# A recurrence done chunk by chunk in PSUM, softplus moved ahead of the pooling, sample taps of the long convolution among the merges, key selection in PSUM

## The chip, the cores and the metric

The program runs on one NeuronCore of a Trainium2 chip. Its engines are TensorE (PE in the profile, with PEld for its weight loads), VectorE (DVE), ScalarE (ACT), GpSimd (POOL) and SyncE (SP), which issues the loads. The metric is the device time of one execution in microseconds; lower is better.

## The reference, cut to what matters

Two layers of a hybrid decoder run over 256 prompt rows and 8 x 4 sample rows, 288 columns in all. In each layer an input projection feeds four mixers, their outputs are gated and merged, and a product-key expert layer (PEER) follows.

```python
# mixer B: trailing means over 2/4/8/16 tokens, minus the token, then a linear per group
# mixer C
xconv = causal_dwconv(ext, w_conv) + b_conv                      # 4 taps, 1024 channels
r  = sigmoid(xh @ w_a + b_a);  ig = sigmoid(xh @ w_i + b_i)
log_a = -8 * r * softplus(-lam);  a = exp(log_a)
bx = sqrt(-expm1(2 * log_a)) * (ig * xconv)
h_t = a_t * h_(t-1) + bx_t                                       # the recurrence
yc = h * gelu(yg)
# mixer D: z = val * sigmoid(gate); 31-tap causal convolution; LayerNorm; silu
# PEER: s = q . keys; top 16 of each half; 16 x 16 sums; top 16 of these;
i1 = take(si[0], pos // 16); i2 = take(si[1], pos % 16); expert = 128 * i1 + i2
```

## The kernel before, in words

Activations lie with channels on the 128 partitions and the 288 columns along the free side. Weights stream from HBM as tiles of 128 output channels: SP loads a tile `raw` (512 KB) into a ring of four. For every half of a tile (4 of 8 blocks of 128x128) ACT writes a rounded high part `w_high`, POOL subtracts it to make `w_low` (line 544), and PE does 12 matmuls of 288 columns (lines 610 to 612: high x high, high x low, low x high). So one tile needs, in this order, two ACT copies, two POOL subtractions and 24 matmuls, and ACT's copy for tile n+2 waits until PE has finished the same half of tile n. ACT also takes each finished tile out of PSUM in order.

The order of all this is written out by hand, per engine, with semaphores: every engine runs its own list in order. In a layer the sections of tiles are B (4 tiles), C (16), S (20 small products with the pool and LRU weights), D (8), A (12), then XB, XC and XA (each pairs of a gate tile and a branch tile), DG, DP, OUT, WQ, U0, KEYS, the U groups and the V groups.

DVE's list in the part that is changed: the norm; wait for B; the pooling of mixer B in four channel groups (lines 1222 to 1236, then the split into `pb_high` and `pb_low`); the argument of softplus (1241, 1243); wait for eight C tiles; the four taps of conv C in PSUM, its sample columns, and the split of `xconv` in four pairs of chunks, each of which raises `c_conv` (line 1258); the softplus series, 24 instructions on 128x8 (1262 to 1283); the split of `y_b`; the products for the recurrence on all eight chunks at once (1290 to 1294); mixer D's gating and sample columns (1297 to 1194); one scan over 2304 elements (1315) and its followers (1317 to 1203); then taps of conv D, most of them between the merges (line 1337) of XB and XC.

PE starts S with waits for `pooled` and for the first `c_conv`. ACT computes the exponential of softplus after its fourth C tile, having waited for DVE's argument (line 911). During D it does Exp and Tanh of each chunk, during A one Sqrt over all chunks (962). `conv_samples` multiplies the window of each sample by the taps and sums.

`route` picks the experts for 128 rows at a time, three times a layer, while PE runs the U groups. With `eq` in SBUF it compares 128 positions with 16 numbers (1517), multiplies by the indices (1520) and sums (1523), each on 128x2048.

Of the kernel before, what the change touches and what calls it, by code (L numbers as in the profile page):

```python
# [37 lines left out]
P = 128  # L38
# [123 lines left out]
def build(nc, w_first, x_in, params_in, final_in, pool_first, ext_in, h0_in, w_in, w_pool, w_lru, w_ab, w_c, w_d, w_out,  # L162
          w_q, w_keys, w_u, w_v, x_keep, y_out, ext_out, h_out):
    with ExitStack() as ctx:
# [140 lines left out]
        lru_exp, lru_ratio, lru_root, y_ready = (sem(n) for n in ("lru_exp", "lru_ratio", "lru_root", "y_ready"))  # L305
        merges_done, chunk_summed, chunk_high = (sem(n) for n in ("merges_done", "chunk_summed", "chunk_high"))
# [149 lines left out]
        with nc.Fori(0, DEPTH) as layer:  # L456
            with nc.Block() as block:
# [146 lines left out]
                def _(pe):  # L604
# [103 lines left out]
                    pe.wait_ge(extra_out, 20)  # L708
# [158 lines left out]
                def _(act):  # L867
# [35 lines left out]
                    for s in range(RING):  # L903
                        into_ext("b", "B", 0, s, s)
                    for g in range(2):
                        for s in range(RING):
                            into_ext("c", "C", g, s, 4 * g + s)
                        if g == 0:

                            act.wait_ge(softplus_arg, 1)  # L910
                            A(lru[:, 1, :], lru[:, 0, :], ACT.Exp, scale=-1.0).then_inc(softplus_exp, 1)
# [28 lines left out]
                    def tanh_of(c0):  # L940
                        for c in (c0, c0 + 1):

                            act.wait_ge(lru_a, c + 1)
                            last = A(rg[:, c, :], rg[:, c, :], ACT.Tanh, scale=lru[:, 7, c:c + 1])
                        return last

                    for s in range(RING):
# [3 lines left out]
                        if s > 0:  # L951
                            last = tanh_of(2 * s - 2)
                    last = tanh_of(CC - 2)
                    last.then_inc(lru_exp, 1)
# [191 lines left out]
                def _(dve):  # L1146
# [22 lines left out]
                    def conv_samples(m, out, bias, scratch, spot):  # L1169
# [3 lines left out]
                        col = PCOL["conv_" + m]  # L1173
                        w, b = spot[:, 0:taps * n], spot[:, taps * n:taps * n + n]
                        did(V.tensor_copy(w, par[:, col:col + taps * n]))
                        if bias:
                            did(V.tensor_copy(b, pcol(bias, 0, n)))
# [3 lines left out]
                        sets = max(1, min(TS, 1152 // size))  # L1181
                        product = [scratch[:, i * size:(i + 1) * size].rearrange("p (c b j) -> p c b j", c=n, b=NB)
                                   for i in range(sets)]
                        s_out = by_seq_all(out)
                        for t0 in range(0, TS, sets):
                            for t in range(t0, t0 + sets):
                                did(V.tensor_tensor(product[t - t0], e[:, :, :, t:t + taps], w, ALU.mult))
                            settle()
                            for t in range(t0, t0 + sets):
                                did(V.tensor_reduce(s_out[:, :, :, t], product[t - t0], AX.X, ALU.add))  # L1190
                            settle()
                        if bias:
                            for t in range(TS):
# [18 lines left out]
                    norm_scale(dve, 0, par[:, PCOL["norm1"]:PCOL["norm1"] + KC])  # L1212
                    dve.wait_ge(padded, 1)
# [27 lines left out]
                    did(V.tensor_scalar(lru[:, 0, :], pcol("lam", 0, CC), -1.0, None, ALU.mult))  # L1241
                    settle()
                    V.tensor_tensor(lru[:, 0, :], lru[:, 0, :], pcol("lam", 0, CC), ALU.max).then_inc(softplus_arg, 1)

# [6 lines left out]
                    conv_samples("c", xconv, "conv_c_b", yb_flat, bank[4])  # L1251
# [9 lines left out]
                    dve.wait_ge(softplus_exp, 1)  # L1261
                    did(V.tensor_scalar(lru[:, 2, :], lru[:, 1, :], 2.0, None, ALU.add))
                    settle()
                    did(V.reciprocal(lru[:, 2, :], lru[:, 2, :]))
                    settle()
                    did(V.tensor_tensor(lru[:, 3, :], lru[:, 1, :], lru[:, 2, :], ALU.mult))
                    settle()
                    did(V.tensor_tensor(lru[:, 4, :], lru[:, 3, :], lru[:, 3, :], ALU.mult))
                    settle()
                    did(V.tensor_scalar(lru[:, 5, :], lru[:, 4, :], 2.0 / 17, 2.0 / 15, ALU.mult, ALU.add))  # L1270
                    for k in (13, 11, 9, 7, 5, 3, 1):
                        settle()
                        did(V.tensor_tensor(lru[:, 5, :], lru[:, 5, :], lru[:, 4, :], ALU.mult))
                        settle()
# [481 lines left out]
```

## Time and profile before

| | us |
|---|---|
| median of 3 runs (lowest, highest) | 2899.95 (2898.25, 2900.65) |
| the profiled execution | 2899.97 |
| its span in the trace | 2898.1 |
| PE, PEld busy | 2670.1, 2621.1 |
| POOL, DVE, ACT busy | 2233.1, 1637.9, 1384.3 |

Times in the rows are counted from the span's start. "Idle before" is how long the engine sat idle ahead of an instruction, with what ended that. PE's matmuls overlap: one lasts 0.30 us and the next starts 0.13 us after it at the full clock, so an idle time read from the profile is 0.17 us shorter than the time that the stall costs.

### The profile page before, as it was taken

Reading aid. Unit: us, or ns where it says so; the run is one execution under the profiler, and the core shown is the slowest. Engines: PE = TensorE matmul, PEld = TensorE weight load, DVE = VectorE, ACT = ScalarE, POOL = GpSimd, SP = SyncE. Lnnn points to the kernel's source line nnn. Section 1 sums busy time; section 2 is a strip of 40 time slices with the busy share of each in tenths; the row PEclk is TensorE's granted clock in tenths of the full one; section 3 lists DMA queues with packets and bytes.
Section 4 is the critical chain, followed back from the end, with each engine's and each line's share of the span. In section 5 each row is a group of like instructions: output and inputs, shape, how many; then the busy total and the mean of one; then the engine's idle time right before and its main releaser. Section 6 shows DMA issues by size and latency. Waiting matters only on the chain. (4 is left out here: it accounts for less than half of the span.)

```text
span 2898.1 us, 58908 instructions
## 1 busy us (share of the span) xinstructions
PE 2670.1 (92%) x19546; PEld 2621.1 (90%) x19546; DVE 1637.9 (57%) x3379; ACT 1384.3 (48%) x2689; POOL 2233.1 (77%) x1819
## 2 busy tenths in 40 slices
PE   7889999999778999999978898999997799999997
PEld 6889889999668999999878898999996699999997
DVE  4686234993885344333656852259928843443336
ACT  4654544445223455554646545444442244554555
POOL 5888667998767878888757876679986678788886
PEclk8999999999999999999989999999999999999999
DMA  4445554454113555555444456545551135555553
GB/s 157 137 137 162 150 167 144 151 160 154 52 38 104 164 154 166 182 166 164 143 137 141 135 156 162 160 139 159 152 152 37 45 123 161 158 161 183 166 166 128
DMA packets 126244, 411.09 MB, mean 142 GB/s; under 512 B 20016, under 2 KB 24496, under 8 KB 125360
## 3 DMA queue, kind: packets, MB, share of 16 engines
q1 hardware_dynamic: 120160, 403.38, 45.3%
q10 hardware_dynamic: 5968, 6.22, 0.9%
q8 instruction: 66, 1.08, 0.2%
q14 instruction: 50, 0.41, 0.0%
HBM read 403.32 MB, written 6.22 MB: 141 GB/s over the span
## 5 line engine op out<-in xcount | busy, mean ns | idle before, releaser
L544 POOL TENSOR_TENSOR w_low<-raw,w_high 128x512 fp32r<-128x512 f32 x1450 | 1987.1, 1379 | 520.3 <-ACT w_high L875 446.4
L875 ACT ACTIVATE w_high<-raw 128x512 fp32r<-128x512 f32 x1266 | 797.0, 633 | 1044.7 <-PE bank L612 1030.0
L610 PE MATMUL bank<-xn_high,w_high 128*128 128x288 f32 x3456 | 1046.6, 303 | 92.8 <-POOL w_low L544 61.7
L611 PE MATMUL bank<-xn_low,w_high 128*128 128x288 f32 x3456 | 1032.4, 299 | 0.0
L612 PE MATMUL bank<-xn_high,w_low 128*128 128x288 f32 x3456 | 1028.2, 298 | 0.0
L610 PEld LDWEIGHTS bank<-xn_high,w_high 128*128 128x128 f32 x3456 | 660.6, 191 | 106.3 <-POOL w_low L544 70.8
L612 PEld LDWEIGHTS bank<-xn_high,w_low 128*128 128x128 f32 x3456 | 662.0, 192 | 0.0
L611 PEld LDWEIGHTS bank<-xn_low,w_high 128*128 128x128 f32 x3456 | 661.2, 191 | 0.2
L1595 DVE TENSOR_TENSOR c_lo<-acts,c_hi 128x288 fp32r<-128x288 f32 x352 | 381.1, 1096 | 446.5 <-ACT c_hi L1089 446.5
L610 PE MATMUL bank<-c_hi,w_high 128*128 128x288 f32 x2048 | 609.1, 297 | 10.0 <-DVE c_lo L1595 9.9
L612 PE MATMUL bank<-c_hi,w_low 128*128 128x288 f32 x2048 | 605.8, 296 | 0.0
L611 PE MATMUL bank<-c_lo,w_high 128*128 128x288 f32 x2048 | 605.2, 296 | 0.0
L610 PEld LDWEIGHTS bank<-c_hi,w_high 128*128 128x128 f32 x2048 | 386.0, 188 | 17.6 <-DVE c_lo L1595 9.8
L611 PEld LDWEIGHTS bank<-c_lo,w_high 128*128 128x128 f32 x2048 | 386.0, 188 | 0.1
L612 PEld LDWEIGHTS bank<-c_hi,w_low 128*128 128x128 f32 x2048 | 385.8, 188 | 0.0
L791 PE MATMUL bank<-one,one 128*128 128x128 f32 x1152 | 167.5, 292 | 91.6 <-issue 50.7
L791 PEld LDWEIGHTS bank<-one,one 128*128 128x128 f32 x1152 | 147.6, 200 | 107.8 <-issue 57.5
L578 POOL TENSOR_SCALAR one<-iota,selT 128x128 f32<-128x128 f32 x288 | 168.0, 601 | 41.7 <-PE bank L791 39.0
L1561 DVE TENSOR_SCALAR one<-bank,selT 128x128 f32<-128x128 f32 x576 | 195.4, 401 | 0.0
L1589 DVE TENSOR_TENSOR acts<-acts,ungated 128x288 f32 x80 | 97.9, 1224 | 153.9 <-ACT ungated L889 153.8
L1098 ACT ACTIVATE w_high<-raw 128x512 fp32r<-128x512 f32 x184 | 115.7, 629 | 112.6 <-PE bank L612 112.6
L1089 ACT ACTIVATE c_hi<-acts 128x288 fp32r (+1 forms) x352 | 146.6, 430 | 22.2 <-PE bank L612 22.2
(237 smaller groups left out, 2431.8 us busy)
## 6 DMA issues: line engine op xcount, KB each, us to landing
raw<-w_u SPq DMA_DIRECT2D x256, 512.0 KB, 3.5
raw<-w_v SPq DMA_DIRECT2D x256, 512.0 KB, 3.5
raw<-w_in_t SPq DMA_DIRECT2D x136, 512.0 KB, 3.5
raw<-w_q SPq DMA_DIRECT2D x32, 512.0 KB, 3.5
raw<-w_ab SPq DMA_DIRECT2D x32, 256.0 KB, 3.1
raw<-w_c SPq DMA_DIRECT2D x16, 512.0 KB, 3.5
raw<-w_out_t SPq DMA_DIRECT2D x16, 512.0 KB, 3.8
raw<-w_first SPq DMA_DIRECT2D x12, 512.0 KB, 3.8
```

The costliest lines, as they stand in the source:

```text
L544: nc.gpsimd.tensor_tensor(w_low[slot][:, :, :], raw[s][:, 4 * half:4 * half + 4, :], w_high[slot][:, :, :].bitcast(F32), ALU.subtract)\
L578: last = nc.gpsimd.tensor_scalar(one1[1][:, t, :], iota[:, :], selT[:, 0, 4 * k + t:4 * k + t + 1], None, ALU.is_equal)
L610: nc.tensor.matmul(out, high, m_high, start=start, stop=False)
L611: nc.tensor.matmul(out, high, m_low, start=False, stop=False)
L612: return nc.tensor.matmul(out, low, m_high, start=False, stop=stop)
L791: last = nc.tensor.matmul(bank[4 + b][:, t * P:(t + 1) * P], one1[b][:, t, :], one2[b][:, t, :], start=True, stop=True)
L875: A(w_high[2 * (s % 2) + half][:, :, :], raw[s][:, 4 * half:4 * half + 4, :], ACT.Copy)\
L1089: A(c_high[:, slot, :], acts[:, i, :], ACT.Copy).then_inc(c_high_out, 1)
L1098: A(w_high[2 * (s % 2) + half][:, :, :], raw[s2][:, 4 * half:4 * half + 4, :], ACT.Copy)\
L1561: last = V.tensor_scalar(one2[b][:, t, :], hot_tiles, selT[:, 1, c:c + 1], selT[:, 2, c:c + 1], ALU.is_equal, ALU.mult)
L1589: V.tensor_tensor(acts[:, 4 * g + s, :], acts[:, 4 * g + s, :], ungated[s], ALU.mult)\
L1595: V.tensor_tensor(c_low[:, slot, :], acts[:, i, :], c_high[:, slot, :].bitcast(F32), ALU.subtract)\
```

## The change

1. The softplus argument and its whole series now stand ahead of the pooling on DVE. ACT computes the exponential right after its first B tile.
2. `ig`: ACT's sigmoid stays in PSUM, and DVE multiplies it by `xconv` from there, chunk by chunk, and only then frees the bank for PE (`extra_out`). The split of `y_b` comes after these eight products.
3. ACT computes `aa` squared into PSUM (banks 5 and 7 in turn) ahead of each Tanh; DVE forms the ratio from there chunk by chunk. Sqrt is done in eight pieces, one after each of the first eight A tiles, from `rg` into PSUM; from the third on it waits until DVE has finished the chunk two before.
4. The recurrence is done per chunk of 288 columns in PSUM: product, first sample states, scan, two copies, product with `yg`, split. It now stands ahead of mixer D's gating. PE waits for its end (`y_ready` of 2) ahead of XB.
5. Conv D: the sample columns move from the D columns to four of the XC merges; XB takes two more taps, and the loop ahead of the merges two fewer. XC's merges are written out instead of looped.
6. `route`: the comparisons, products and sums run on 128x512 pieces in banks 4 and 5, with the 16 numbers in bank 7.

```diff
@@ tensor
-                    pe.wait_ge(extra_out, 20)
+                    pe.wait_ge(y_ready, 2)
                     branch("XB", "b")
@@ scalar
                     for s in range(RING):
                         into_ext("b", "B", 0, s, s)
-                    for g in range(2):
-                        for s in range(RING):
-                            into_ext("c", "C", g, s, 4 * g + s)
-                        if g == 0:
+                        if s == 0:
 
                             act.wait_ge(softplus_arg, 1)
                             A(lru[:, 1, :], lru[:, 0, :], ACT.Exp, scale=-1.0).then_inc(softplus_exp, 1)
...
-                                    ins = A(ig[:, c, :], src, ACT.Sigmoid, bias=pcol("bi", c))
-                                ins.then_inc(extra_out, 1)
+                                    ins = A(src, src, ACT.Sigmoid, bias=pcol("bi", c))
+                                ins.then_inc(extra_out if s < 2 else ig_ready, 1)
...
                             act.wait_ge(lru_a, c + 1)
-                            last = A(rg[:, c, :], rg[:, c, :], ACT.Tanh, scale=lru[:, 7, c:c + 1])
+                            if c > 1:
+                                act.wait_ge(lru_ratio, c - 1)
+                            A(bank[5 + c % 2 * 2][:, 0:T], aa[:, c, :], ACT.Square)
+                            A(rg[:, c, :], rg[:, c, :], ACT.Tanh, scale=lru[:, 7, c:c + 1]).then_inc(lru_exp, 1)
...
-                            if (g, s) == (0, 3):
-                                act.wait_ge(lru_ratio, 1)
-                                A(rg, rg, ACT.Sqrt).then_inc(lru_root, 1)
+                            c = 4 * g + s
+                            if c < CC:
+                                act.wait_ge(lru_ratio, CC)
+                                if c > 1:
+                                    act.wait_ge(scanned, c - 1)
+                                A(bank[5 + c % 2 * 2][:, 0:T], rg[:, c, :], ACT.Sqrt).then_inc(lru_root, 1)
@@ vector
                     norm_scale(dve, 0, par[:, PCOL["norm1"]:PCOL["norm1"] + KC])
+                    did(V.tensor_scalar(lru[:, 0, :], pcol("lam", 0, CC), -1.0, None, ALU.mult))
+                    settle()
+                    V.tensor_tensor(lru[:, 0, :], lru[:, 0, :], pcol("lam", 0, CC), ALU.max).then_inc(softplus_arg, 1)
+
+                    dve.wait_ge(softplus_exp, 1)
+                    did(V.tensor_scalar(lru[:, 2, :], lru[:, 1, :], 2.0, None, ALU.add))
...
+                    V.tensor_scalar(lru[:, 7, :], lru[:, 5, :], LRU_C, None, ALU.mult).then_inc(softplus_done, 1)
...
-                    dve.wait_ge(lru_exp, 1)
-                    did(V.tensor_tensor(ig, ig, xconv, ALU.mult))
-                    settle()
-                    did(V.tensor_tensor(xconv, aa, aa, ALU.mult))
-                    settle()
-                    V.scalar_tensor_tensor(rg, xconv, 1.0, rg, ALU.add, ALU.mult).then_inc(lru_ratio, 1)
+                    for c in range(CC):
+                        dve.wait_ge(ig_ready, c + 1)
+                        V.tensor_tensor(ig[:, c, :], bank[4 + c % 4][:, 0:T], xconv[:, c, :], ALU.mult).then_inc(extra_out, 1)
+                    split(y_b, "b", y_ready)
...
+                    for c in range(CC):
+                        state = lru_bank(c)
+                        by_seq_state = by_seq(state)
+                        dve.wait_ge(lru_root, c + 1)
+                        did(V.tensor_tensor(state, state, ig[:, c, :], ALU.mult))
...
+                        did(V.tensor_tensor_scan(state, aa[:, c, :], state, 0.0, ALU.mult, ALU.add))
...
+                        did(V.tensor_tensor(state, state, yg[:, c, :], ALU.mult))
...
+                        did(V.tensor_copy(yc_high[:, c, :], state))
...
+                    V.sem_inc(y_ready, 1)
...
-                    early = CONV["d"] - 1 - 3 * KC
+                    early = CONV["d"] - 1 - 3 * KC - 2
...
+                    for c in range(KC):
+                        merge("XC", c // 2, 2 * (c % 2) + 1, [next_tap, next_tap + 1])
+                        next_tap += 2
+                        if c == 2:
+                            sample_weights("d", "conv_d_b", spot)
+                        if 2 < c < 3 + TS:
+                            conv_samples("d", cd, "conv_d_b", prod_flat, spot, c - 3, c - 2)
@@ route
-                        for c in range(2):
-                            did_r(V.tensor_tensor(e3, posf[:, c, :].unsqueeze(2).to_broadcast([P, HK, TOPK]),
-                                                iota16[:, :].unsqueeze(1).to_broadcast([P, HK, TOPK]), ALU.is_equal))
...
+                                e3 = bank[4 + q % 2][:, :].rearrange("p (s j) -> p s j", j=TOPK)
+                                did_r(V.tensor_tensor(e3, posf[:, c, h * TOPK:(h + 2) * TOPK].unsqueeze(2)
+                                                      .to_broadcast([P, 2 * TOPK, TOPK]),
+                                                      iota16_here.unsqueeze(1).to_broadcast([P, 2 * TOPK, TOPK]), ALU.is_equal))
```

On DVE, at the seam between the layer's norm and the pooling (`xn_low` is the last of the norm, `win` the window sums of the pooling), before:

```order
L371 TENSOR_TENSOR xn_low<-xnf,xn_high 128x288 x2
L1222 TENSOR_TENSOR win_99<-ext_b 128x422
L1230 SCALAR_TENSOR_TENSOR p_b<-win_99,ext_b 128x240
L1232 SCALAR_TENSOR_TENSOR p_b<-win_99,ext_b 128x32
L1234 TENSOR_TENSOR p_b<-win_99,first_cnt 128x16
```

The same place now, with the middle of the series left out:

```order
L372 TENSOR_TENSOR xn_low<-xnf,xn_high 128x288 x2
L1220 TENSOR_SCALAR lru<-par 128x8
L1222 TENSOR_TENSOR lru<-lru,par 128x8
L1225 TENSOR_SCALAR lru<-lru 128x8
L1227 RECIPROCAL lru<-lru 128x8
...
L1243 TENSOR_TENSOR lru<-lru 128x8
L1245 TENSOR_SCALAR lru<-lru 128x8
L1246 TENSOR_SCALAR lru<-lru 128x8
L1257 TENSOR_TENSOR win_99<-ext_b 128x422
L1265 SCALAR_TENSOR_TENSOR p_b<-win_99,ext_b 128x240
```

26 small instructions stand now where the pooling began at once.

On DVE, between conv C's split and mixer D's gating (`yb` is mixer B's output, `h0a` the incoming sample states), before:

```order
L1201 CAST yb_high<-y_b 128x1152
L1203 TENSOR_TENSOR yb_low<-y_b,yb_high 128x1152
L1290 TENSOR_TENSOR ig<-ig,xconv 128x2304
L1292 TENSOR_TENSOR xconv<-aa 128x2304
L1294 SCALAR_TENSOR_TENSOR rg<-xconv,rg 128x2304
L1297 TENSOR_TENSOR ext_d<-d_val,d_gate 128x4x256
L1298 TENSOR_TENSOR ext_d<-d_val,d_gate 128x4x8x4
...
L1162 TENSOR_SCALAR bank<-ext_d,par 128x256 x4
L1306 TENSOR_TENSOR ig<-ig,rg 128x2304
```

Now, to the end of the first of eight chunks:

```order
L1295 TENSOR_TENSOR ig<-bank,xconv 128x288 x8
L1208 CAST yb_high<-y_b 128x1152
L1210 TENSOR_TENSOR yb_low<-y_b,yb_high 128x1152
L1303 SCALAR_TENSOR_TENSOR rg<-bank,rg 128x288 x8
...
L1316 TENSOR_TENSOR bank<-bank,ig 128x288
L1318 TENSOR_TENSOR bank<-bank,h0a 128x8
L1320 SCALAR_TENSOR_TENSOR bank<-aa,bank 128x288
L1322 COPY h_last<-bank 128x1
L1323 COPY h_last<-bank 128x8
L1325 TENSOR_TENSOR bank<-bank,yg 128x288
L1327 CAST yc_high<-bank 128x288
L1329 TENSOR_TENSOR yc_low<-bank,yc_high 128x288
```

The instructions on 128x2304 are gone, eight groups of eight on one chunk stand in their place, and mixer D's gating comes behind all of them.

On ACT, the second tile of D, with Exp of chunks 2 and 3 and Tanh of chunks 0 and 1 (`aa` is a, `rg` is r), before:

```order
L875 ACTIVATE w_high_57<-raw_54 128x512
L875 ACTIVATE w_high_58<-raw_54 128x512
L889 ACTIVATE d_val<-bank 128x288
L950 ACTIVATE aa<-rg,lru 128x288 x2
L944 ACTIVATE rg<-rg,lru 128x288 x2
```

In the same tile now:

```order
L876 ACTIVATE w_high_57<-raw_54 128x512
L876 ACTIVATE w_high_58<-raw_54 128x512
L890 ACTIVATE d_val<-bank 128x288
L953 ACTIVATE aa<-rg,lru 128x288 x2
L947 ACTIVATE bank<-aa 128x288
L948 ACTIVATE rg<-rg,lru 128x288
L947 ACTIVATE bank<-aa 128x288
L948 ACTIVATE rg<-rg,lru 128x288
```

Two Squares into PSUM are added in each such tile.

## Rows read from the trace of the kernel before

**Rows 1.** The page's busy times, whole span

```profile
PE 2670.1 (92%) x19546; PEld 2621.1 (90%) x19546; DVE 1637.9 (57%) x3379; ACT 1384.3 (48%) x2689; POOL 2233.1 (77%) x1819
```

**Rows 2.** PE's waits in 60:70, 97:110, 125:141, 158:190 and 500:720

```profile
PE bank L610 <- POOL w_low L544: 5.1, 1, 5.1
...
PE bank L610 <- POOL w_low L544: 2.0, 2, 1.5
PE bank L610 <- ACT rg L930: 1.7, 1, 1.7
...
PE bank L610 <- POOL w_low L544: 4.4, 3, 1.7
...
PE bank L610 <- POOL w_low L544: 7.3, 4, 3.3
...
PE bank L610 <- POOL w_low L544: 8.8, 9, 1.4
```

**Rows 3.** Windows by engine: busy time, PE's granted clock, DMA

```profile
60.00:67.00 7.00, 5.14 (x21) 5.14 (x22) 0.00 (x0) 3.38 (x9) 6.05 (x5) 0.52 0.32 81
158.00:172.00 14.00, 8.92 (x56) 8.44 (x56) 13.88 (x9) 3.90 (x8) 14.00 (x6) 0.91 0.22 73
```

**Rows 4.** POOL's line 544: ns minimum/median/maximum of all its instructions

```profile
L544 POOL TENSOR_TENSOR w_low<-raw,w_high x1450: 1260/1293/5908, 28.9 to 2875.8; 128x512 fp32r<-128x512 f32 x182
```

**Rows 5.** Timeline of DVE, 125:180: start, duration, idle before

```profile
125.44 2.56 DVE L1290 TENSOR_TENSOR ig<-ig,xconv 128x2304 f32<-128x2304 f32 x1 [17.91 <-ACT rg L944]
...
162.18 5.77 DVE L1315 TENSOR_TENSOR_SCAN xconv<-aa,ig 128x2304 f32<-128x2304 f32 x1
```

**Rows 6.** Routing on DVE, 480:680, groups by form: count, busy, mean ns

```profile
L1517 DVE TENSOR_TENSOR eq<-posf,iota 128x2048 f32<-128x2048 f32 x6 | 19.8, 3298 | 0.2
```

**Rows 7.** Timeline of POOL and DVE, 47.5:49.5

```profile
47.90 1.32 POOL L544 TENSOR_TENSOR w_low<-raw,w_high 128x512 fp32r<-128x512 f32 x1 [0.21 <-ACT w_high L875]
...
47.98 1.27 DVE L1234 TENSOR_TENSOR p_b<-win,first_cnt 128x16 f32<-128x16 f32 x1
49.29 0.17 DVE L1236 TENSOR_TENSOR p_b<-p_b,ext_b 128x16 f32<-128x16 f32 x1
49.38 0.59 DVE L1222 TENSOR_TENSOR win<-ext_b 128x422 f32<-128x422 f32 x1
```

**Rows 8.** Timeline of DVE from the first pooling instruction, 38:54

```profile
38.72 1.67 DVE L1222 TENSOR_TENSOR win<-ext_b 128x422 f32<-128x422 f32 x1 [10.86 <-ACT ext_b L901]
...
50.01 3.17 DVE L1222 TENSOR_TENSOR win<-win 128x420 f32<-128x420 f32 x2
```

**Rows 9.** Timeline of DVE, conv C, its split, and softplus, 71:105

```profile
71.90 3.68 DVE L1162 TENSOR_SCALAR bank<-ext_c,par 128x256 f32<-128x256 f32 x8 [12.19 <-ACT ext_c L901]
...
91.14 1.85 DVE L1258 TENSOR_TENSOR xc_low<-xconv,xc_high 128x576 fp32r<-128x576 f32 x1
...
97.85 1.25 DVE L1262 TENSOR_SCALAR lru<-lru 128x8 f32<-128x8 f32 x1
...
104.36 0.17 DVE L1283 TENSOR_SCALAR lru<-lru 128x8 f32<-128x8 f32 x1
```

**Rows 10.** Timeline of ACT: first B tile, softplus's exponential, last C tile, D

```profile
31.23 0.19 ACT L901 ACTIVATE ext_b<-bank 128x32 f32<-128x32 f32 x1
...
59.74 0.21 ACT L911 ACTIVATE lru<-lru 128x8 f32<-128x8 f32 x1 [7.07 <-DVE lru L1243]
...
97.01 0.39 ACT L889 ACTIVATE yg<-bank 128x288 f32<-128x288 f32 x1
...
115.33 1.14 ACT L875 ACTIVATE w_high<-raw 128x512 fp32r<-128x512 f32 x2
...
117.52 0.95 ACT L944 ACTIVATE rg<-rg,lru 128x288 f32<-128x288 f32 x2
```

**Rows 11.** DVE's line 1337, one chunk with one operand in PSUM

```profile
L1337 DVE TENSOR_TENSOR bank<-bank,gates x32: 466/467/467, 233.5 to 1757.3; 128x288 f32<-128x288 f32 x32
```

**Rows 12.** DVE's waits in 500:720

```profile
DVE denom L1536 <- ACT routed L1050: 42.1, 1, 42.1
```

More of the change, by code:

```diff
@@ L904, in _ @@
                         into_ext("b", "B", 0, s, s)
+                        if s == 0:
+                            act.wait_ge(softplus_arg, 1)
+                            A(lru[:, 1, :], lru[:, 0, :], ACT.Exp, scale=-1.0).then_inc(softplus_exp, 1)
                     for g in range(2):
@@ L951, in _ @@
                         if s > 0:
-                            last = tanh_of(2 * s - 2)
-                    last = tanh_of(CC - 2)
-                    last.then_inc(lru_exp, 1)
+                            tanh_of(2 * s - 2)
+                    tanh_of(CC - 2)
                     for s in range(RING):
@@ L1167, in conv_tap, with sample_weights @@
                         return tap
-                    def conv_samples(m, out, bias, scratch, spot):
+                    def sample_weights(m, bias, spot):
+                        n, taps = CHUNKS[m], CONV[m]
+                        col = PCOL["conv_" + m]
+                        did(V.tensor_copy(spot[:, 0:taps * n], par[:, col:col + taps * n]))
+                        if bias:
+                            did(V.tensor_copy(spot[:, taps * n:taps * n + n], pcol(bias, 0, n)))
+                        settle()
@@ L1178, in conv_samples @@
-                        settle()
                         w = w.rearrange("p (j c) -> p c j", c=n).unsqueeze(2).to_broadcast([P, n, NB, taps])
                         size = n * NB * taps
-                        sets = max(1, min(TS, 1152 // size))
-                        product = [scratch[:, i * size:(i + 1) * size].rearrange("p (c b j) -> p c b j", c=n, b=NB)
-                                   for i in range(sets)]
+                        product = {t: scratch[:, (t - t0) * size:(t - t0 + 1) * size]
+                                   .rearrange("p (c b j) -> p c b j", c=n, b=NB) for t in range(t0, t1)}
@@ L1184, in conv_samples @@
                         s_out = by_seq_all(out)
-                        for t0 in range(0, TS, sets):
-                            for t in range(t0, t0 + sets):
-                                did(V.tensor_tensor(product[t - t0], e[:, :, :, t:t + taps], w, ALU.mult))
-                            settle()
-                            for t in range(t0, t0 + sets):
-                                did(V.tensor_reduce(s_out[:, :, :, t], product[t - t0], AX.X, ALU.add))
-                            settle()
+                        for t in range(t0, t1):
+                            did(V.tensor_tensor(product[t], e[:, :, :, t:t + taps], w, ALU.mult))
@@ L1192, in conv_samples @@
+                        settle()
+                        for t in range(t0, t1):
+                            did(V.tensor_reduce(s_out[:, :, :, t], product[t], AX.X, ALU.add))
+                        settle()
                         if bias:
-                            for t in range(TS):
+                            for t in range(t0, t1):
                                 did(V.tensor_tensor(s_out[:, :, :, t], s_out[:, :, :, t],
@@ L1272, in _ @@
+                    settle()
+                    did(V.memset(by_seq_all(aa)[:, :, :, 0], 0.0))
+                    did(V.memset(aa[:, :, 0:1], 0.0))
+                    yc_high, yc_low = pair["c"]
+                    for c in range(CC):
+                        state = lru_bank(c)
+                        by_seq_state = by_seq(state)
+                        dve.wait_ge(lru_root, c + 1)
+                        did(V.tensor_tensor(state, state, ig[:, c, :], ALU.mult))
                         settle()
-                        did(V.tensor_tensor(lru[:, 5, :], lru[:, 5, :], lru[:, 4, :], ALU.mult))
+                        did(V.tensor_tensor(by_seq_state[:, :, 0], by_seq_state[:, :, 0], h0a[:, c, :], ALU.add))
```

129 lines of the change are left out of this document (63 added, 66 removed).

## The prediction, made before the changed kernel ran

> **What bounds the kernel now.** The page comes first: PE is busy for 92% of the span, POOL for 77%, DVE for 57% and ACT for 48% [rows 1]. PE is the bound wherever it doesn't wait, so the question is where it waits. PE's waits, taken stretch by stretch, name POOL's `w_low` nearly everywhere: 5.1 us ahead of the seventh C tile, 2.0 in S, 4.4 in D, 7.3 in A, and 8.8 in nine pieces during routing; one more in S, 1.7, is ACT's [rows 2]. The same stretches of the second layer show the same numbers. Each piece costs 0.17 us more than it shows: 5.3, 2.3, 4.9, 8.0 and 10.3 us.
>
> POOL itself is not slow. Its median is 1.29 us, so two halves take 2.6 of the 3.2 us that a tile takes on PE; the longest is 5.9 us [rows 4]. That one starts when DVE's scan of 5.77 us runs [rows 5]. So the next view is POOL beside DVE. Where DVE works from SBUF to SBUF with two inputs, the two take turns: a DVE instruction of 16 columns started 0.08 us into a POOL one took 1.27 us and ended 0.03 us after it, while the like one behind it, with POOL idle, took 0.17 [rows 7]. Products of 2048 columns in routing take 3.3 us for the same reason, and hold POOL in turn [rows 6]. DVE's taps and merges with one operand in PSUM show no such lengthening: 466 to 467 ns, smallest to largest, though POOL works beside them [rows 11].
>
> The wait ahead of the seventh C tile is another thing: ACT stood 7.07 us in its list for the softplus argument [rows 10], which DVE makes only after its pooling. No weights were split meanwhile.
>
> After long waits PE runs at half clock for a while: granted 0.52 in 60:67, and 0.91 in 158:172 [rows 3]. Half clock spaces matmuls by 0.24 instead of 0.13 us; the 21 of 60:67 lose 2.3 us, and 0.09 x 2 x 14 = 2.5 us at half clock in A lose 1.3 us.
>
> **Routing.** The four products of 2048 columns in each third of the routing become sixteen of 512 with one operand in PSUM. They no longer take turns with POOL, and the nine waits go: 10.3 us per layer. The new time on DVE is hidden: it waits 42.1 us for ACT after its last selection [rows 12], so three times the pieces at a fixed cost of 0.1 to 0.2 us each (18 more instructions, under 4 us) are covered. If that cover were gone, nothing would change until 42 us were used.
>
> **Recurrence and A.** The scan and its five companions on 2304 columns hold POOL through A. In chunks, all but two 64-column instructions have at most one SBUF tensor, so the 8.0 us and the 1.3 us of slow clock go: 9.3 us. What comes instead is pace. ACT's Sqrt for chunk c waits for chunk c-2. A chunk takes the 0.47 us of a chunk product [rows 11] five times (two products, cast and subtraction, and the scan at 0.8, by 5.77 less a turn of about 1 us over eight), 0.2 for the sample states, 0.3 for two copies: some 3.4 us, against 3.2 per tile. The eight chunks start at tile 0 and need be kept two apart, which allows 3.2 x 7/6 = 3.7 us. So ACT never waits. PE's wait ahead of XB: the eighth chunk ends some 30 us into A, and A lasts 38.4 us. Mixer D's gating and five taps (20 instructions of about 0.45 us and 3 us of gating: 12 us) then end just as XB's first merge is due, 43 us into it. The sample columns add a product and a sum of 992 columns to each of four XC merges, some 2.5 us by the columns of [rows 11]; PE lets merges lag by two, 12.8 us, which covers all four. Nothing for these; without that cover they would cost 10 us. Bounds of this term: 6 to 10 us.
>
> **D.** The three products that held POOL there (the first is in [rows 5]) become chunk products from PSUM. The 4.9 us go. But ACT gets eight Squares in D's first four tiles. A tile there took ACT 3.04 us (from 115.33 to 118.37) with Exp and Tanh at 0.43 us each [rows 10]; two Squares at 0.35 to 0.43 make it 3.8, over PE's 3.2. ACT falls 3 us further behind, and its lead of about 1 us over the point at which POOL's second half comes late turns into one stall of 2 us. The split of `y_b` now falls beside the first D tiles and takes two turns from POOL: 0.6 us. Gain 2.3 us, bounds 0 to 4.5.
>
> **B, C and S, the part that decides.** PE no longer stands ahead of the seventh C tile: 5.3 + 2.3 = 7.6 us. DVE's wait of 10.86 us ahead of the pooling [rows 8] looks like room for the softplus series. ACT can load the table and compute Exp from 31.4 on, after the first B tile [rows 10], so the 24 small instructions start near 33. Before, they took from 97.85 to 104.5 [rows 9], 6.7 us, with POOL mostly idle. Now POOL is catching up on B and C. While it runs back to back, one small instruction fits behind each POOL one (1.25 us); by about 43.5 eleven are through. Then POOL pauses 0.2 to 0.3 us in each 1.6, and two or three fit: thirteen more take 6.5 us. The series ends near 50.
>
> The pooling follows. Of its 28 instructions, 14 ran beside POOL from 38.72 to 53.18 [rows 8], 1.03 us each; the other 14 ran in 6.5 us until 59.7 (71.90 less 12.19 [rows 9]), since POOL had nothing to do while ACT stood. That cover is gone: POOL now works throughout, so all 28 go at about 1 us. Pooling ends near 78, against 59.7. Its slack was up to the eighth C tile, which is now at 64.
>
> Conv C is then late. From its first tap to the first `c_conv` it took 71.90 to 92.99, 21.1 us [rows 9], less 2 us of turns now that POOL will run dry: `c_conv` at 97.1. PE finishes C 7.6 us sooner than before, or 7.0 with 0.6 lost at the third B tile, where the table load delays a split: at 89.9 instead of 96.9 (ACT took the last C tile at 97.01 [rows 10]). So it waits 7.2 us and starts S when it started before. The wait costs half clock again, 2.1 us, part of which S's own waits absorb; S's waits shrink by 0.5 us, as the split of `y_b` no longer meets POOL there. Net: -1.6 us per layer. Bounds: +8 (series and pooling fit) to -8 (each ten us later).
>
> **A rule weighed.** The Trainium skill, page SBUF — State Buffer, section Who interferes with whom, says that a DVE instruction with two SBUF inputs and a GpSimd one that reads SBUF exclude each other for the whole instruction, and that one with a single SBUF input outside the two-port modes doesn't contend. The trace agrees on both [rows 7, 11]. Its exclusive hold, taken to the letter with no overlap at a change of hands, is rival 2.
>
> **The sum.** Per layer 10.3 + 9.3 + 2.3 - 1.6 = 20.3; two layers 40.6. The profiled execution took 2899.97 (span 2898.1 and 1.9 around it), which is the median of the three runs within 0.02. Forecast: 2859.4 us.
>
> **Rivals.**
> 1. The series and the pooling fit into DVE's idle time. For it: 10.9 + 12.2 us of idle time stand there [rows 8, 9]. Against: the 14 instructions at 1.03 us. PE then neither waits nor slows at S: 7.2 + 2.1 + 0.6 = 9.9 per layer more: 2839.6. Chance 0.13.
> 2. No overlap at a change of hands. With POOL back to back a turn then costs 0.1 to 0.2 us more twice over, POOL's lag never drains, and one DVE instruction per POOL one is all: 21 x 1.4 = 29 us for the series, 32 for the pooling, 94 instead of 78. 16 us per layer less: 2891. Against it: 1.27 us of duration that ends 0.03 us behind POOL's with 0.17 of its own [rows 7]. By the page's letter this is the case. Chance 0.06.
> 3. The chunks set A's pace. Over 3.7 us each, PE loses seven times the excess; at 5 us 9 per layer: 2878. Chance 0.05.
> 4. Slower than before: each of the 52 instructions waits out a whole half tile, 1.6 us, as no pause is ever free. 33 + 83 = 116 for the pooling, S at 135, 38 us per layer later: 2935. It decides from 20 us per layer beyond my 78, that is a pooling that ends past 98. Against it: two instructions in one pause [rows 7]. Chance 0.05.
> 5. PSUM operands don't free POOL: DVE and POOL take turns as before: about 2899. [rows 11] speak against it. Chance 0.02.
>
> **How the numbers follow.** The forecast case has 0.69, its own range 2848 to 2871 from the bounds of its terms. The range given, 2840 to 2878, takes rival 1 at its lower end and rival 3 at its upper; outside are rivals 2, 4, 5 and edges, below 0.2. Under 0.2% (6 us) a measurement of this kernel can't tell from no change. Faster 0.92 (forecast, 1 to 3 without the tail), same 0.03, slower 0.05.
>
> **What would show it.** The wait for `c_conv` (PE idle ahead of S for 5 to 10 us, DVE as releaser) and the pooling's end near 78; no wait ahead of the seventh C tile; no PE wait on `w_low` in routing; one of some 2 us in D; none in A; POOL's maximum at 3 us or below in A. An S that starts at once, or one later than 105, makes the forecast wrong.

## The result, and the profile after

The changed kernel took 2852.85 us (median of 4 runs, 2851.45 to 2860.18), the one before 2899.1 in the same comparison (2897.24 to 2900.65). The ratio is 0.9845, interval 0.9830 to 0.9859. The forecast was 2859.4, with a range of 2840 to 2878. The profiled execution took 2853.29 us, its span 2851.4: 46.7 us off the span, where the sum had 40.6.

PE now works 93% of a shorter span, and POOL is busy for 78 us less [rows 1 for before]:

```profile
PE 2658.5 (93%) x19546; PEld 2616.8 (92%) x19546; DVE 1645.4 (58%) x3627; ACT 1392.9 (49%) x2719; POOL 2154.7 (76%) x1819
```

PE's waits answer to [rows 2]. The windows are 90:100, 100:115 and 125:141, in this order; 26:40 has 0.5 and 115:125 has 0.4 us on `w_low` besides:

```profile
PE bank L611 <- issue: 9.7, 1, 9.7
...
PE bank L611 <- POOL w_low L545: 1.5, 1, 1.5
PE bank L611 <- ACT rg L931: 0.4, 1, 0.4
...
PE bank L611 <- POOL w_low L545: 1.4, 1, 1.4
```

60:90, 141:192 and 440:705 show no wait of PE at all. The waits ahead of the seventh C tile, in A and in routing are gone, and one of 9.7 us stands ahead of S. The profile calls its releaser "issue", because the semaphore from DVE doesn't show. DVE's timeline names it: the first pair of the conv's result is split at 98.23 + 0.75 = 98.98, and PE starts S at 99.08. Timeline of DVE in the kernel after, from the softplus argument's answer to the i gate's products:

```profile
32.83 0.17 DVE L1225 TENSOR_SCALAR lru<-lru 128x8 f32<-128x8 f32 x1 [4.79 <-ACT lru L909]
...
33.47 1.23 DVE L1231 TENSOR_TENSOR lru<-lru 128x8 f32<-128x8 f32 x1
34.73 1.22 DVE L1233 TENSOR_SCALAR lru<-lru 128x8 f32<-128x8 f32 x1
...
49.97 0.16 DVE L1246 TENSOR_SCALAR lru<-lru 128x8 f32<-128x8 f32 x1
50.04 0.59 DVE L1257 TENSOR_TENSOR win<-ext_b 128x422 f32<-128x422 f32 x1
...
80.00 3.67 DVE L1167 TENSOR_SCALAR bank<-ext_c,par 128x256 f32<-128x256 f32 x8
...
98.23 0.75 DVE L1290 TENSOR_TENSOR xc_low<-xconv,xc_high 128x576 fp32r<-128x576 f32 x1
...
108.83 1.63 DVE L1295 TENSOR_TENSOR ig<-bank,xconv 128x288 f32<-128x288 f32 x4 [7.11 <-ACT bank L933]
```

An instruction on 8 columns from SBUF to SBUF takes 0.17 us alone and 1.2 where it waits for POOL. The series runs from 32.83 to 50.13, the pooling from 50.04 to 80.00. Behind the wait PE runs at half clock for a while: the window 99:107 of the kernel after shows a granted clock of 0.66. The window 158:172, in A, shows 1.00, where it was 0.91 in [rows 3]:

```profile
99.00:107.00 8.00, 7.48 (x36) 7.31 (x37) 2.73 (x5) 6.13 (x13) 1.28 (x1) 0.66 0.11 22
158.00:172.00 14.00, 14.00 (x107) 14.00 (x106) 12.98 (x35) 7.57 (x16) 11.16 (x10) 1.00 0.48 134
```

One chunk of the recurrence, and POOL's instructions from 142 to 180 (least, median, longest in ns), against the scan in [rows 5] and the 5908 ns in [rows 4]:

```profile
161.65 0.45 DVE L1316 TENSOR_TENSOR bank<-bank,ig 128x288 f32<-128x288 f32 x1
...
162.34 0.76 DVE L1320 TENSOR_TENSOR_SCAN bank<-aa,bank 128x288 f32<-128x288 f32 x1
...
164.40 0.46 DVE L1329 TENSOR_TENSOR yc_low<-bank,yc_high 128x288 fp32r<-128x288 f32 x1
164.78 0.45 DVE L1316 TENSOR_TENSOR bank<-bank,ig 128x288 f32<-128x288 f32 x1
...
L545 POOL TENSOR_TENSOR w_low<-raw,w_high x24: 1279/1292/2373, 141.1 to 177.8; 128x512 fp32r<-128x512 f32 x24
```

A chunk takes 164.78 - 161.65 = 3.13 us. In routing, the key selection's comparisons in DVE's groups of 480:700, and DVE's wait behind its last selection (window 500:720), answer to [rows 6, 12]:

```profile
L1542 DVE TENSOR_TENSOR bank<-posf,bank 128x512 f32<-128x512 f32 x24 | 15.5, 692 | 0.4
...
DVE denom L1570 <- ACT routed L1055: 40.7, 1, 40.7
```

**Where the time went.** Both traces have 19546 matmuls, so each has its partner. The table gives the start of the same matmul in both:

```
matmul, layer 1                  before   after    lead   gained since
first of D                       108.72  111.95   -3.2   -3.2  (B, C, S)
one tile behind D's last wait    137.95  138.31   -0.4   +2.9  (D)
one tile behind A's last wait    181.50  171.91   +9.6   +9.9  (A)
first of the delta gate          329.89  318.57  +11.3   +1.7
behind the last routing wait     679.65  655.27  +24.4  +13.1  (11.1 of it in the three thirds)
```

Layer 2 gives -3.3, +2.9, +10.0, +1.9 and +10.4 by the same matmuls; its three thirds of routing give 11.1 too. The slow clock behind the gate's wait is counted in the last row; with it the gate's own gain is 3.3 us in layer 1 and 1.7 in layer 2.

### The profile page after: what moved, and what is told of

The parts are those of the page before. It is cut to its first block and busy times, and to the rows that moved or that the text cites. A ratio compares the mean times of both kernels' runs of the same rounds, so it can differ in the third digit from the quotient of the medians.

```text
span 2851.4 us, 59032 instructions
## 1 busy us (share of the span) xinstructions
PE 2658.5 (93%) x19546; PEld 2616.8 (92%) x19546; DVE 1645.4 (58%) x3627; ACT 1392.9 (49%) x2719; POOL 2154.7 (76%) x1819
## 5 line engine op out<-in xcount | busy, mean ns | idle before, releaser
L545 POOL TENSOR_TENSOR w_low<-raw,w_high 128x512 fp32r<-128x512 f32 x1450 | 1908.6, 1323 | 551.9 <-ACT w_high L876 477.3
L611 PEld LDWEIGHTS bank<-c_hi,w_high 128*128 128x128 f32 x2048 | 385.5, 188 | 17.5 <-DVE c_lo L1629 10.0
```

Of the source, the lines that this page charges most:

```text
L545: nc.gpsimd.tensor_tensor(w_low[slot][:, :, :], raw[s][:, 4 * half:4 * half + 4, :], w_high[slot][:, :, :].bitcast(F32), ALU.subtract)\
L611: nc.tensor.matmul(out, high, m_high, start=start, stop=False)
```

## The experiments

Each ratio is against the kernel before on the same chip; the kernel after has 0.9845. The kernel before took 2897.47 us beside experiments 1 to 4, 2898.49 beside 5 to 8 and 2900.45 beside 9 to 11, so times of different experiments can be compared only to some 3 us. Matmul starts come from one execution of each kernel. Edits are to the kernel after where nothing else is said.

**1. The series with its scratch in a PSUM bank.** Is the series long because of POOL?

```diff
-did(V.tensor_scalar(lru[:, 5, :], lru[:, 5, :], 2.0 / k, None, ALU.add))
+did(V.tensor_scalar(ser[:, 5, :], ser[:, 5, :], 2.0 / k, None, ALU.add))   # ser is in bank 7
```

> The kernel after, with the scratch rows of the softplus series in a PSUM bank: of its 24 small instructions only one still has two SBUF inputs, the others have one operand or the result in PSUM. Theory (turns with POOL): the series took 17.2 us because POOL holds the way to SBUF; it now takes about 6 us (24 at 0.2 us, one turn), the pooling ends near 69 instead of 80.0, the first c_conv comes near 88, before PE has done with C (89.1), so PE neither waits nor slows ahead of S: 10 to 12 us per layer, 2830 us, 2826 to 2838. Rival (the series is long by its own chain of dependent instructions or by its place in the list, not by POOL): nothing changes, 2853. Half of the 24 still slow would mean that an instruction with one SBUF input and its result in PSUM takes turns too: pooling near 74, some 2843.

Measured: 2835.94 us, 0.9793 (0.9776 to 0.9809). Timeline of DVE in this kernel, and of PE's waits in 85:110 the one ahead of S:

```profile
32.83 0.17 DVE L1226 TENSOR_SCALAR bank<-lru 128x8 f32<-128x8 f32 x1 [5.84 <-ACT lru L909]
...
33.48 1.22 DVE L1232 TENSOR_TENSOR lru<-lru 128x8 f32<-128x8 f32 x1
34.73 0.17 DVE L1234 TENSOR_SCALAR bank<-lru 128x8 f32<-128x8 f32 x1
...
38.41 0.15 DVE L1247 TENSOR_SCALAR lru<-bank 128x8 f32<-128x8 f32 x1
...
88.64 1.85 DVE L1291 TENSOR_TENSOR xc_low<-xconv,xc_high 128x576 fp32r<-128x576 f32 x1
...
PE bank L611 <- issue: 1.2, 1, 1.2
```

The one instruction that keeps two SBUF inputs (L1232) is the one that still takes 1.2 us; an SBUF input with a PSUM result (L1234) takes 0.17. The series ends at 38.56 in place of 50.13, and PE starts S at 90.59 in place of 99.08. That is 8.5 us per layer, and 9.9 at the first matmul of D, where the slow clock that no longer follows is counted in. It is just under my 10 to 12: the split's first piece met POOL (1.85 us for 0.75), and 1.2 us of wait stayed. The rival falls. The medians give 16.9 us for both layers.

**2. The series back in its old place, argument and Exp early.** The block from L1224 to L1246 moves behind the conv's split.

> The kernel after, with the argument and the Exp early as now, but the series of 22 small instructions back in its old place behind the split of the conv's result. Theory: the pooling starts near 33 instead of 50 and ends near 63, c_conv is ready before PE has done with C, and PE doesn't wait ahead of S (10 to 12 us per layer). The series then runs beside POOL at about 1.2 us an instruction from 87 or so to about 105, with the i gate's products and the split of y_b behind it; D's first Exp needs it near 107. If it is in time: 2832 us; if ACT has to wait for it in D, up to 2 us per layer of that come back: 2836. Rival (the series costs its 10 us wherever it stands, once it runs beside POOL): 2853.

Measured: 2843.53 us, 0.9821 (0.9799 to 0.9843). PE starts S at 90.60, as in 1, but DVE's timeline and the longest of PE's waits in 90:112 show what follows:

```profile
94.25 1.23 DVE L1270 TENSOR_SCALAR lru<-lru 128x8 f32<-128x8 f32 x1
...
95.74 0.17 DVE L1274 TENSOR_TENSOR lru<-lru 128x8 f32<-128x8 f32 x1
...
101.92 1.54 DVE L1295 TENSOR_TENSOR ig<-bank,xconv 128x288 f32<-128x288 f32 x4
...
PE bank L611 <- DVE ig L1295: 3.6, 1, 3.6
```

POOL had caught up there, so the series took 8 us and not 18. The time is above my 2832 to 2836 all the same, because PE, in S, waits 3.6 us for the banks of the i gate, since the products that free them stand behind the series. I had looked at ACT in D as the one who waits; it was PE in S.

**3. Only the key selection changed, in the kernel before.**

> The kernel before with nothing but the key selection changed (sixteen products of 512 columns with an operand in PSUM in place of four of 2048). Theory: the nine waits of routing go, 10.3 us per layer: 2878.5 us, within 3; the waits in C, S, D, A and ahead of the first tile of the delta gate (3.8 us) stay. Rival (that stretch is helped by what the other edits do to POOL earlier): the waits stay, 2899.

Measured: 2879.06 us, 0.9931 (0.9910 to 0.9951). PE shows no wait from 500 to 710, and the first tile of the delta gate is still waited for (3.4 us between two starts). By matmul starts the three thirds gain 11.1 us in each layer, exactly as in the kernel after, so this gain is the selection's own. The medians give 18.4 us for both layers.

**4. Only recurrence, i gate's products and sample columns changed.** Softplus and key selection stand as before.

> The kernel after with softplus and key selection as in the kernel before, so that the recurrence by chunks, the i gate's products and the moved sample columns are alone. Theory: 9.3 us in A and 2.3 in D per layer, 23 in all: 2876 us. If the 1.8 us per layer by which PE waits less ahead of the delta gate's first tile, which was not forecast, belong to this part, 2872; if they belong to another part, 2876 with a wait of 3.8 us there. Rival (the gain in A comes from the time that PE lost earlier, not from the chunks): A's waits of 8 us are back, 2890 or more.

Measured: 2875.71 us, 0.9922 (0.9905 to 0.9940). PE's waits in 60:70, 125:190 and 480:700:

```profile
PE bank L611 <- POOL w_low L545: 5.1, 1, 5.1
...
PE bank L611 <- POOL w_low L545: 1.4, 1, 1.4
...
PE bank L611 <- POOL w_low L545: 8.8, 9, 1.4
```

A is free of waits and D keeps one of 1.4 us; the waits in C and in routing stay as they were in [rows 2]. By matmul starts, 1.1 us come in S, 2.9 in D and 9.9 in A: 13.9 per layer for my 11.6. The rival falls.

**5. Only argument and Exp early, in the kernel before.**

> The kernel before with only the softplus argument ahead of the pooling and its Exp behind the first B tile; series, recurrence and key selection as before. Theory: PE's wait ahead of the seventh C tile and the slow clock behind it go (7.6 us per layer), but the pooling now runs beside POOL all the way and the conv's result comes at about 90.5, so 1.5 us of wait and 1 us of slow clock come at S. The shorter wait ahead of the delta gate's first tile, seen in every kernel with the early argument (2.0 for 3.8 us), comes with it: 6.9 us per layer, 2885 us. Without that part 2889. Rival: the conv's result comes no later than before, 9.4 us per layer: 2880.

Measured: 2891.41 us, 0.9975 (0.9965 to 0.9984). The wait ahead of the seventh C tile is gone, and by matmul starts the lead over the kernel before is 6.75 us behind it and the slow clock that followed it, 5.4 at S, where 1.2 us of wait have come, and 5.5 at D's end; D shows 4.3 us of waits, as before. In layer 1 the delta gate's first tile is waited for nearly as long as before (3.64 us between two starts for 3.81), but in layer 2 it is 2.46 for 4.24. My 2885 fell, the 2889 without the shorter wait is near; whether the early argument shortens it is not settled by this run.

**6. The Squares behind D's tiles 4 to 7.**

```diff
 step("D", 1, s, d_gate[:, s, :], ACT.Sigmoid)
+for c in (2 * s, 2 * s + 1):
+    if c > 1: act.wait_ge(lru_ratio, c - 1)
+    A(bank[5 + c % 2 * 2][:, 0:T], aa[:, c, :], ACT.Square).then_inc(lru_exp, 1)
```

> The kernel after, with the eight Squares moved on ACT from D's first four tiles to behind its tiles 4 to 7, where ACT stands 0.7 to 0.9 us per tile. Theory (ACT's eight Squares of 0.40 us make the wait of 1.69 us in D): the wait goes, the one of 0.65 ahead of the first D tile stays, 1.8 us per layer: 2849 us. The last ratio comes some 2 us into A, where the first Sqrt waits for it behind the second A tile at the earliest; should ACT fall behind there, a wait of 1 to 2 us in A takes its place: 2853. Rival (the wait in D is POOL's turns with the split of y_b): it stays, 2853.

Measured: 2853.08 us, 0.9837 (0.9820 to 0.9853). PE's waits in 115:190 and in 310:320:

```profile
PE bank L611 <- POOL w_low L545: 0.4, 1, 0.4
...
PE bank L611 <- POOL w_low L545: 3.0, 1, 3.0
```

The wait of 1.4 us in D is gone, so it was the Squares', and none came in A. Nothing of it reaches the end in layer 1: ahead of the delta gate PE waits 3.0 us in place of 1.7, and that matmul starts at 318.60, with the kernel after at 318.57. In layer 2 the same wait is short, 1.84 us between two starts.

**7. The recurrence's scratch in SBUF, chunks as they are.**

```diff
-    return bank[5 + c % 2 * 2][:, 0:T]
+    return xconv[:, c, :]     # and the same in ACT's Square and Sqrt
```

> The kernel after, with the scratch of the recurrence (square, root and state of a chunk) in SBUF, in the place that the conv's result no longer needs, in place of two PSUM banks; chunks and order as in the kernel after. Theory (an operand in PSUM is what frees POOL): each of the ten instructions of a chunk then waits out a POOL one, about 1.25 us each, and holds POOL in turn; a chunk takes 10 to 13 us in place of 3.1, the loop 80 to 105 us in place of 25, and DVE is 50 to 70 us late for XB's first merge: 2950 to 2990 us. If only half of them take turns: near 2880. Rival (the gain is that the pieces are short): the chunks fit between POOL's halves, 2853 to 2857.

Measured: 2886.20 us, 0.9954 (0.9938 to 0.9971), 33 us slower than the kernel after, and far from my 2950. Timeline of DVE, of POOL and of ACT in one chunk, and PE's waits in 155:192:

```profile
158.20 0.76 DVE L1320 TENSOR_TENSOR_SCAN xconv<-aa,xconv 128x288 f32<-128x288 f32 x1
...
159.07 0.98 DVE L1323 COPY h_last<-xconv 128x8 f32<-128x8 f32 x1
160.08 1.50 DVE L1325 TENSOR_TENSOR xconv<-xconv,yg 128x288 f32<-128x288 f32 x1
...
158.73 2.53 POOL L545 TENSOR_TENSOR w_low<-raw,w_high 128x512 fp32r<-128x512 f32 x2 [2.29 <-ACT w_high L876]
...
157.69 0.44 ACT L967 ACTIVATE xconv<-rg 128x288 f32<-128x288 f32 x1 [3.07 <-DVE yc_low L1329]
...
PE bank L611 <- POOL w_low L545: 6.5, 5, 1.4
PE bank L611 <- DVEq L1332: 4.1, 1, 4.1
```

A chunk takes 4.83 us (L1325 starts at 155.26, 160.08 and 164.91). It meets two POOL instructions, not ten: ACT stands 3.07 us for the chunk two before, its splits come late, and POOL is idle for 2.29 us of each round, in which DVE's instructions with two SBUF inputs run at their own length. This is the prediction's rival 3, made real: once chunks are slower than tiles, chunk, root and weight split go round in one ring, and PE loses about 1.5 us a tile. Rival 3's own rule, seven times the excess over 3.7 us, gives 7.9 us; A's gain fell from 9.9 to 2.2, by 7.7. The 4.1 us on L1332 are PE's wait for the end of the chunks, ahead of XB. So the operand in PSUM is needed in A. My estimate failed because it let POOL run on.

**8. The key selection's pieces of 512 in SBUF.**

```diff
-e3 = bank[4 + q % 2][:, :].rearrange("p (s j) -> p s j", j=TOPK)
+e3 = eq[:, q % 2 * 512:q % 2 * 512 + 512].rearrange("p (s j) -> p s j", j=TOPK)
```

> The kernel after, with the key selection's sixteen products of 512 columns per third on SBUF tiles in place of PSUM banks. Theory: each takes a turn with POOL and holds it for 0.6 us; sixteen hold it 9 us in some 8 tiles, where it has 0.6 us to spare per tile and a buffer ahead: PE loses 2 to 3 us per third, 6 to 9 per layer: 2865 to 2872 us. Rival (short pieces are enough): no wait in routing, 2853.

Measured: 2870.82 us, 0.9895 (0.9879 to 0.9912). The size was as expected, the place was not. DVE's groups in 480:700, ACT's exponential behind the selection, PE's waits in 440:720, and DVE's wait behind its last selection:

```profile
L1542 DVE TENSOR_TENSOR eq<-posf,iota 128x512 f32<-128x512 f32 x24 | 37.1, 1585 | 0.4
...
701.44 0.52 ACT L1055 ACTIVATE routed<-routed 128x384 f32<-128x384 f32 x1 [6.88 <-DVE routed L1558]
...
PE bank L611 <- POOL w_low L545: 5.2, 1, 5.2
...
DVE denom L1568 <- ACT routed L1055: 0.6, 1, 0.6
```

The nine waits don't come back, and the three thirds gain the same 11.1 us as in the kernel after: short pieces alone let POOL keep its lead. But each of the 48 comparisons and products takes 0.9 us more (1585 for 692 ns), 44 us in all, and this uses up the 40.7 us for which DVE stood behind its last selection. ACT, which stands 6.88 us for the last selection, splits no weights meanwhile, and PE waits once, 5.2 us and its slow clock. So it was the length of a piece that freed POOL here, and the operand in PSUM that kept DVE in time.

**9. Series and last window sum in PSUM, Squares late.** The last window sum of each pooled chunk goes to `bank[5 + c % 2]`.

> The kernel with the series in PSUM (2836), and besides: the last window sum of each pooled chunk goes to a PSUM bank, so that the twelve instructions that read it have one SBUF input; and the Squares behind D's tiles 4 to 7. Theory: the pooling took 27 us from 39.36 beside POOL; its twelve readers take no turn any more, some 8 to 10 us less, so the conv's result comes near 82, 7 us before PE has done with C, and its split is over before S's turns matter. PE's wait of 1.49 us ahead of S and the slow clock in S go, 2 to 3.5 us per layer, and the wait of 1.7 in D goes, while the wait ahead of the delta gate's first tile may be 3.3 us in place of 2.2, as with the Squares alone. 2829 us, 2824 to 2834. Rival (what PE waits for at S is no longer the conv's result): 2836.

Measured: 2835.01 us, 0.9770 (0.9750 to 0.9789); not told apart from experiment 1. The stretches did what was said, if less: the conv's first piece is split at 86.2 (I had 82; the sums keep two SBUF inputs and 1.57 us each), S starts as PE ends C, 1.1 us sooner than in 1, and with D's wait gone the lead over 1 is 2.4 us behind D and 2.9 at the end of routing. Between the matmuls that start at 754 and 854 it falls to -0.2. There PE runs at half clock now and then, in other places from kernel to kernel (754:780 has a granted clock of 0.92 here and 1.00 in experiment 1); why is open. From the end of layer 1's routing to the start of layer 2, matmuls that start 0.18 to 0.30 us after the one before, for 0.13 at the full clock, lose 18.9 us here and 16.2 in experiment 1. Behind the routing of layer 2 they lose 17.5 and 14.2, and the lead is lost again. So a gain of some 3 us found early in a layer can't be seen in the time of the whole.

**10. Three of ACT's five stores early.** What does PE wait for ahead of the delta gate? Timeline of ACT's queue, kernel before and, below the dots, after:

```profile
322.75 2.73 ACTq L993 DMA_DIRECT2D ext_out_a<-ext_a  x1
325.64 2.10 ACTq L994 DMA_DIRECT2D h_out<-h_last  x1
327.87 1.15 ACT L875 ACTIVATE w_high<-raw 128x512 fp32r<-128x512 f32 x2 [6.64 <-issue]
...
313.29 1.51 ACTq L998 DMA_DIRECT2D ext_out_a<-ext_a  x1
314.97 1.44 ACTq L999 DMA_DIRECT2D h_out<-h_last  x1
316.54 1.15 ACT L876 ACTIVATE w_high<-raw 128x512 fp32r<-128x512 f32 x2 [4.79 <-issue]
```

> The kernel after, with three of ACT's five DMAs of the layer's states taken out of the place ahead of the delta gate: the ones of mixers B and C are issued beside A's tiles 9 and 10, the one of the last states behind XB. The first theory, that the shorter wait there comes with the early argument, has fallen: one kernel with it waited 3.64 us, and the kernel with the late Squares 3.33. Theory now: PE waits there for as long as ACT is held by its five issues (4.8 us in the kernel after, 6.6 in the one before) less some 2.8 us of lead, whatever sets their length. With two issues left ACT is held for 2.5 us or less, and the wait goes: 1.97 us and some slow clock, 2 to 3 us per layer: 2848 us. Rival (one issue is long because the queue is full of earlier descriptors, so that fewer take as long): nothing changes, 2853. A third outcome: the stores beside A hold ACT there for more than its 0.9 us of idle time, and PE loses 1 us each: 2851.

Measured: 2850.15 us, 0.9820 (0.9804 to 0.9836). PE shows no wait in 300:320, and the two stores that stay are issued in 0.57 and 0.55 us each. By matmul starts 1.7 us are gained in layer 1 and 2.3 more in layer 2. The runs' medians differ by 2.7 us, too little to tell by themselves.

**11. All of it together.**

> Both together: series and last window sum in PSUM, Squares behind D's tiles 4 to 7, three of the five stores early. If the parts add up: 2829 less 4 to 8: 2823 us, 2817 to 2830. If the stores give nothing: 2829.

Measured: 2826.72 us, 0.9744 (0.9727 to 0.9760): 26 us below the kernel after. It is 8.3 us below experiment 9, but the early stores are not worth that much by themselves: 6.3 us of the lead over 9 come between the routing of layer 1 and the start of layer 2, where the two kernels do the same and the widely spaced matmuls lose 13.7 us for 18.9. PE's waits in 85:125, all that is left there:

```profile
PE bank L611 <- POOL w_low L545: 1.9, 2, 1.5
PE bank L611 <- ACT rg L931: 1.7, 1, 1.7
```

## Why the prediction was right, step by step

**Routing, 10.3 per layer: 11.1 measured, as an effect of the selection** (experiment 3). The nine waits are 10.2 of it; the other 0.9 is half clock behind them, which the prediction left out here though it counted it in A. The mechanism was half right. The prediction put it all to turns with POOL; pieces of 512 that still take turns remove the nine waits as well (8). It called DVE's added time covered; it was, and used 1.4 of the 42.1 us, but only because the pieces run at 0.69 us and not at 1.6.

**A, 9.3 per layer: 9.9 measured**, and 9.9 again alone (4). Chunks took 3.13 us for my 3.4, though the parts that I listed add up to 3.2; the scan, which I put at 0.8 (5.77 less 1 over eight is 0.6), took 0.76. ACT never waited as long as one stayed under 3.7; at 4.83 it did, with the ring that rival 3 described (7). POOL's longest in A was 2.37 us, under the 3 that I gave. XB's first merges and the moved sample columns cost nothing, as said: PE has no wait up to 200.

**D, 2.3 per layer: 2.9.** Two gaps between matmul starts, of 0.65 and 1.69 us, stand for my 0.6 and 2. The Squares make the second (6). That the split of `y_b` makes the first was not tested.

**B, C and S, -1.6 per layer: -3.2.** This term was mis-sized by the pooling and by the end of C. The series ended at 50.13, forecast 50. The 28 pooling instructions took 29.96 us and not 28: the pooling ended at 80.0 for my 78, the conv's result came at 98.98 for 97.1. PE was also done with C earlier than I had it: in the kernel before S starts at 96.27, where I had read 96.9 from ACT. So PE stood 9.9 us for 7.2. The matmuls of 90:115, spaced by half clock, lost 2.7 us where 0.4 were lost before: 2.3 for my 2.1. S's own waits fell from 3.2 to 1.9 us, 1.3 for my 0.5, and not by the step that I gave. I had expected the split of `y_b` to leave POOL alone; the wait for POOL is 1.5 us as before, and it is the one for ACT that fell, from 1.7 to 0.4. In experiment 1, where PE doesn't run slowly there, it is 1.4. So the slow clock is in part made up for by a wait that gets shorter, as the prediction said without a size. That the series and its turns are the cause is shown by experiment 1. Against the recurrence alone (4), whose matmul behind A's last wait starts at 167.57, the moved softplus costs 4.3 us per layer up to A's end (171.91); with the scratch in PSUM (162.03) it gives 5.5.

By the Trainium skill (page SBUF — State Buffer, section Who interferes with whom) a DVE instruction with a single SBUF input outside the two-port modes doesn't contend with GpSimd. Experiment 1 agrees, with 0.17 us for L1234 beside POOL. In the kernel after the same instruction with its result in SBUF (L1233) took 1.22 us; whether it ran in a two-port mode no trace shows, so it speaks neither for the rule nor against it. The prediction's rival 2, an exclusive hold with no overlap at the change of hands, would have ended the pooling at 94; it ended at 80.0.

**Not in the sum: the wait ahead of the delta gate, 1.8 and 1.9 us shorter in the two layers; with the slow clock behind it 3.3 and 1.7.** That PE waits there for as long as ACT is held by its five stores is shown by 10, where two stores are left and the wait is gone. Why the last two stores take 4.8 us to issue in one kernel and 3.0 in another is open. First I put it to the early argument. Layer 1 of 5 and 6 speaks against that (3.64 and 3.33 us between two starts), layer 2 of the same runs for it: there every kernel with the early argument that still has its five stores at the gate waits 1.8 to 2.9 us, and the three without it 3.0 to 4.2. The loads on SP's queue were issued at the same distance in both kernels, to 0.1 us.

**The balance.** The sum was short by 6.1 us, and behind this stand errors of both signs. Over two layers B, C and S gave 3.3 us less than forecast; D and A gave 2.5 more, routing 1.6 more, and the gate, at nothing in the sum, 5.0. So the largest error is known by place, not by cause. That the total came out this near is in part luck.

## What to carry to other kernels

Before moving a chain of small DVE instructions into idle time, look at what POOL does there: beside a busy POOL the series took 17.3 us, and 5.7 with its scratch in PSUM. Test apart whether a long instruction hurts by its length or by its turns with POOL. In routing short pieces alone took PE's waits away (8). In A they did not, because a chunk in SBUF took longer than a tile and ACT stood for it (7). In both places the operand in PSUM kept DVE in time. When a stall goes, ask who profited from it: here half of the pooling had run fast because POOL had nothing to do while ACT stood.

## What the runs showed that was not expected

- A DVE instruction of 8 columns with one SBUF input and an SBUF result takes 1.22 us beside POOL (L1233), and 0.17 with the result in PSUM (L1234 of experiment 1).
- Where DVE, ACT, POOL and PE waited for each other in a ring, ten DVE instructions that could have taken turns met only two POOL ones per chunk, since POOL stood idle for 2.29 us of each round (7).
- The store of mixer A's state took ACT's queue 1.51 us to issue in one kernel, 2.73 in another, and 0.55 when only one store stood before it (10).
